# Value products of two attention groups from neighbouring tokens, the residue and class order made by a store and a load

## The reference

```python
def dilated_group(q, k, v, bias_table, window, dilation):
    # query t attends keys t - j*dilation, 0 <= j*dilation <= window
    ...
    s = jnp.einsum('brnqhe,brnkhe->brnhqk', qb, kb) * (E ** -0.5) + bias
    ...
    o = jnp.einsum('brnhqk,brnkhe->brnqhe', p, vb)
    o = o / den
...
for g, (window, dilation) in enumerate(DILATED_GROUPS):
    q, k, v = three projections of u for this group, 2048 columns each
    o, lse = dilated_group(q, k, v, table, window, dilation)
wts = softmax over the groups' lse
o = sum of wts * o;  y = o * silu(gate);  return y @ w_out
```

## Time and profile before

| | us |
|---|---|
| median of 3 timed runs (lowest, highest) | 1629.93 (1629.87, 1630.2) |
| profiled execution, whole | 1630.79 |
| its span | 1629.1 |
| TensorE busy with products | 1615.5 |
| TensorE busy with weight loads | 1372.4 |
| VectorE / ScalarE / GpSimd busy | 809.1 / 643.3 / 97.1 |

### The profile page before, as it was taken

One profiled execution on the slowest core, in us unless ns is written; L12 is line 12 of the kernel. 1 busy time (PEld: TensorE's weight loads), 2 busy tenths in 40 slices (PEclk: granted clock), 3 DMA queues, 4 the chain that ended last, 5 costly groups with the idle time before them and its releaser, 6 DMA issues.

```text
span 1629.1 us, 23054 instructions
## 1 busy us (share of the span) xinstructions
PE 1615.5 (99%) x8584; PEld 1372.4 (84%) x8584; DVE 809.1 (50%) x1452; ACT 643.3 (39%) x1096; POOL 97.1 (6%) x166
## 2 busy tenths in 40 slices
PE   9999999999999999999999999999999999999997
PEld 7888888888887998888998888898888889888886
DVE  6874674575677724444333444423344431443446
ACT  7553453453453533333232334332333332243332
POOL 5600000000000020000020000002000001000000
PEclk9999999999999999999999999999999999999999
DMA  6623223223221444333242343334423333433311
GB/s 181 185 81 98 77 77 95 85 77 90 78 78 52 122 125 97 84 83 84 65 142 79 96 97 84 71 102 118 96 62 89 94 71 104 133 95 86 83 50 65
DMA packets 251265, 151.99 MB, mean 93 GB/s; under 512 B 49536, under 2 KB 230352, under 8 KB 251184
## 3 DMA queue, kind: packets, MB, share of 16 engines
q1 hardware_dynamic: 204592, 138.95, 30.8%
q0 software_dynamic: 4592, 11.09, 2.0%
q10 hardware_dynamic: 42000, 0.79, 1.4%
HBM read 144.30 MB, written 5.71 MB: 92 GB/s over the span
## 4 chain that ended last, share of the span: by engine, by line
PE 97%; DVE 2%; ACT 1%; DMA 1%; issue 0%; DVEq 0%; ACTq 0%; SPq 0%
PE proj L475 81%; PE inner L794 3%; PE inner L475 3%; PE inner L742 1%; PE inner L777 1%; PE inner L760 1%; PE inner L658 1%; PE inner L681 1%; PE inner L684 1%; PE inner L670 1%; PE inner L663 0%; PE inner L756 0%; DMA ident<-consts 0%; DVE v L1702 0%; DMA stat_o<-residue_stats 0%; PE inner L691 0%
## 5 line engine op out<-in xcount | busy, mean ns | idle before, releaser
L1214 DVE TENSOR_TENSOR w_lo<-raw,w_hi 128x1024 fp32r<-128x1024 f32 x252 | 307.8, 1222 | 443.1 <-ACT w_hi L843 442.2
L475 PE MATMUL proj<-u_hi,w_hi 128*128 128x512 f32 x1280 | 509.5, 398 | 0.0
L475 PE MATMUL proj<-u_hi,w_lo 128*128 128x512 f32 x1280 | 499.6, 390 | 0.0
L475 PE MATMUL proj<-u_lo,w_hi 128*128 128x512 f32 x1280 | 498.5, 389 | 0.0
L843 ACT ACTIVATE w_hi<-raw 128x1024 fp32r<-128x1024 f32 x252 | 265.0, 1052 | 129.9 <-PE proj L475 116.7
L475 PEld LDWEIGHTS proj<-u_hi,w_lo 128*128 128x128 f32 x1280 | 240.2, 188 | 52.0
L475 PEld LDWEIGHTS proj<-u_lo,w_hi 128*128 128x128 f32 x1280 | 240.7, 188 | 48.0
L475 PEld LDWEIGHTS proj<-u_hi,w_hi 128*128 128x128 f32 x1280 | 240.5, 188 | 48.1 <-issue 0.3
L475 PE MATMUL proj<-w_hi,u_hi 128*128 128x512 f32 x440 | 176.9, 402 | 0.2 <-DVE u_lo L1278 0.2
L475 PE MATMUL proj<-w_hi,u_lo 128*128 128x512 f32 x440 | 173.6, 394 | 0.0
L475 PE MATMUL proj<-w_lo,u_hi 128*128 128x512 f32 x440 | 173.5, 394 | 0.0
(11 more groups left out here) (189 smaller groups left out, 1547.2 us busy)
## 6 DMA issues: line engine op xcount, KB each, us to landing
raw<-at_w_in SPq DMA_DIRECT2D x160, 512.0 KB, 4.3
raw<-hg_w_in SPq DMA_DIRECT2D x63, 512.0 KB, 4.1
raw<-hg_w_out SPq DMA_DIRECT2D x16, 512.0 KB, 3.6
raw<-at_w_out SPq DMA_DIRECT2D x16, 512.0 KB, 4.2
v<-rows POOLq DMA_DIRECT2D x64, 64.0 KB, 2.0
v<-x SPq DMA_DIRECT2D x4, 512.0 KB, 6.0
bias_tiles<-ext_rows POOLq DMA_DIRECT2D x1, 2048.0 KB, 11.1
bias_n<-bias_tiles POOLq DMA_DIRECT2D x16, 128.0 KB, 4.5
```

The lines of the kernel that those rows point to most:

```text
L475: ins = nc.tensor.matmul(bank[:, :], stationary(a), moving(b), start=(first and n == 0), stop=(last and n == 2))
L1214: nc.vector.tensor_tensor(w["lo"][:, slot, :], raw[:, slot, :], w["hi"][:, slot, :].bitcast(F32), ALU.subtract).then_inc(w_ready, 1)
```

## The change

The value products of all three groups take tokens 128s to 128s + 127. The order that groups 2 and 3 want is made afterwards: ScalarE writes each block to a row of `rows` (`staged`), GpSimd stores it to a DRAM tensor, in token order, and when a group's four blocks are stored, one transfer of 1 MB loads them with token 4i + r on partition i and in block r (group 2), or with the classes one behind the other (group 3). Since the RMS factor now goes by token for both groups, VectorE makes it in one order only. New waits: ScalarE's, for the store that last read the row; GpSimd's, for a group's four stores; and VectorE's, before it writes a quad's first logits over the rows.

```diff
+        turn_dram = nc.dram_tensor("value_rows", [GROUPS - 1, S, HQ * P], F32, kind="Internal").ap()
...
-        staged_v = rows[:, 8:10, :]
+        def staged(q, group, s):
+
+            if q is None:
+                return rows[:, 4 + s if group == 1 else 8 + s if s < 2 else 2 + s, :]
+            return rows[:, 8 + s % 2, :]
...
-            def move_classes(q):
-
+            turned = (None, turn_dram[0].rearrange("(i r) n -> i (r n)", r=RES),
+                      turn_dram[1].rearrange("(m c r) n -> c m (r n)", c=CLASSES, r=RES))
+
+            def turn_rows(q, group):
+
+                turn = 0 if q is None else q + 1
                 for s in range(ST):
-                    _, bank, filled = AT.event(q, 2 * ST + s + (0 if q is None else AT.heads))
+                    _, bank, filled = AT.event(q, ST * group + s + (0 if q is None else AT.heads))
                     wait_turn(pool, pool_met, bank_free[bank], filled + 1)
-                    for c in range(CLASSES):
-                        pool.dma_start(v_sb[2][c * MEM:(c + 1) * MEM, s, :], staged_v[c::CLASSES, s % 2, :])\
-                            .then_inc(v_moved[s % 2], 16)
-
-            move_classes(None)
+                    if q is not None and s == 0:
+                        wait_turn(pool, pool_met, v_loaded[group], turn * 16)
+                    pool.dma_start(turn_dram[group - 1, s * P:(s + 1) * P, :], staged(q, group, s))\
+                        .then_inc(v_stored[group][s], 16)
+                for stored in v_stored[group]:
+                    wait_turn(pool, pool_met, stored, (turn + 1) * 16)
+                pool.dma_start(v_sb[group][:, :, :].rearrange("p a b -> p (a b)"), turned[group]).then_inc(v_loaded[group], 16)
+
+            turn_rows(None, 1)
+            turn_rows(None, 2)
...
                 if not last:
-                    move_classes(q)
+                    turn_rows(q, 1)
+                    turn_rows(q, 2)
...
-                        cols = slice(s, S, RES) if group else slice(s * P, (s + 1) * P)
+                        cols = slice(s * P, (s + 1) * P)
...
-                cols = slice(s, S, RES) if group else slice(s * P, (s + 1) * P)
+                cols = slice(s * P, (s + 1) * P)
...
                 if h == 0:
-                    for moved in v_moved:
-                        pe.wait_ge(moved, (g // HQ + 1) * 2 * 16 * CLASSES)
+                    for loaded_rows in v_loaded[1:]:
+                        pe.wait_ge(loaded_rows, (g // HQ + 1) * 16)
...
-            def move_values(q, e, s, bank):
+            def stage_values(q, group, e, s, bank):
 
                 turn = 0 if q is None else q + 1
-                if s >= 2 or q is not None:
-                    act.wait_ge(v_moved[s % 2], (2 * turn + s // 2) * 16 * CLASSES)
-                nc.scalar.activation(staged_v[:, s % 2, :], value_bank(AT, q, e)[:, :], ACT.Copy).then_inc(bank_free[bank], 1)
+                if q is None and group == 2 and s >= 2:
+                    act.wait_ge(v_stored[1][s - 2], 16)
+                elif q is not None and s >= 2:
+                    act.wait_ge(v_stored[group][s - 2], (turn + 1) * 16)
+                elif q is not None and group == 1:
+                    act.wait_ge(v_stored[2][s + 2], turn * 16)
+                elif q is not None:
+                    act.wait_ge(v_stored[1][s + 2], (turn + 1) * 16)
+                raw_u = q is None and group == 1
+                nc.scalar.activation(staged(q, group, s), value_bank(AT, q, e)[:, :], ACT.Copy,
+                                     scale=cols[:, 8 + s:9 + s] if raw_u else 1.0).then_inc(bank_free[bank], 1)
...
-            picked = (y_f, eg)
-            for i, row in enumerate((rstd[:, :].rearrange("p (t n) -> p t n", t=ST),
-                                     rstd[:, :].rearrange("p (n r) -> p r n", r=RES))):
...
+            picked = y_f[:, :].rearrange("p (t n) -> p t n", t=ST)
+            nc.vector.tensor_tensor(picked, rstd[:, :].rearrange("p (t n) -> p t n", t=ST),
+                                    ident[:, :].unsqueeze(1).broadcast_to([P, ST, P]), ALU.mult).then_inc(rcol_step, 1)
...
+                        if i == K1 and h == 0:
+                            for loaded_rows in v_loaded[1:]:
+                                dve.wait_ge(loaded_rows, (q + 1) * 16)
```

More of the change, by code:

```diff
@@ L270, in program @@
         spread_out = sem("spread_out")
-        v_moved = [sem(f"v_moved{i}") for i in range(2)]
+        v_stored = [None] + [[sem(f"v{g}_stored{s}") for s in range(ST)] for g in range(1, GROUPS)]
+        v_loaded = [None] + [sem(f"v{g}_loaded") for g in range(1, GROUPS)]
         fin_T, fin_base, fin_sq, fin_step, fin_rstd, fin_ready = sems("fin_T fin_base fin_sq fin_step fin_rstd fin_ready")
@@ L850, in copy_values @@
                 raw_u = q is None and group < 2
-                if layer is AT and group == 2:
-                    move_values(q, e, s, bank)
+                if layer is AT and group:
+                    stage_values(q, group, e, s, bank)
                     return
                 nc.scalar.activation(v_sb[group][:, s, :], value_bank(layer, q, e)[:, :], ACT.Copy,
-                                     scale=cols[:, 8 + ST * group + s:9 + ST * group + s] if raw_u else 1.0)\
+                                     scale=cols[:, 8 + s:9 + s] if raw_u else 1.0)\
                     .then_inc(bank_free[bank], 1)
-            def move_values(q, e, s, bank):
+            def stage_values(q, group, e, s, bank):
                 turn = 0 if q is None else q + 1
-                if s >= 2 or q is not None:
-                    act.wait_ge(v_moved[s % 2], (2 * turn + s // 2) * 16 * CLASSES)
-                nc.scalar.activation(staged_v[:, s % 2, :], value_bank(AT, q, e)[:, :], ACT.Copy).then_inc(bank_free[bank], 1)
+                if q is None and group == 2 and s >= 2:
[9 more added lines that the diff above has]
+                                     scale=cols[:, 8 + s:9 + s] if raw_u else 1.0).then_inc(bank_free[bank], 1)
             def u_high(which, k):
@@ L1552, in _ @@
             dve.wait_ge(rstd_ready, 2)
-            picked = (y_f, eg)
-            for i, row in enumerate((rstd[:, :].rearrange("p (t n) -> p t n", t=ST),
-                                     rstd[:, :].rearrange("p (n r) -> p r n", r=RES))):
-                nc.vector.tensor_tensor(picked[i][:, :].rearrange("p (t n) -> p t n", t=ST), row,
-                                        ident[:, :].unsqueeze(1).broadcast_to([P, ST, P]), ALU.mult).then_inc(rcol_step, 1)
-            for i in range(2):
-                dve.wait_ge(rcol_step, i + 1)
-                ins = nc.vector.tensor_reduce(cols[:, 8 + ST * i:8 + ST * (i + 1)],
-                                              picked[i][:, :].rearrange("p (t n) -> p t n", t=ST), AX.X, ALU.add)
-            ins.then_inc(rcol_ready, 1)
+            picked = y_f[:, :].rearrange("p (t n) -> p t n", t=ST)
+            nc.vector.tensor_tensor(picked, rstd[:, :].rearrange("p (t n) -> p t n", t=ST),
+                                    ident[:, :].unsqueeze(1).broadcast_to([P, ST, P]), ALU.mult).then_inc(rcol_step, 1)
+            dve.wait_ge(rcol_step, 1)
+            nc.vector.tensor_reduce(cols[:, 8:8 + ST], picked, AX.X, ALU.add).then_inc(rcol_ready, 1)
             split_lo(AT, None, 3, False)
```

## The result

| | before | after |
|---|---|---|
| median of 9 runs, us (lowest, highest) | 1629.97 (1629.25, 1631.51) | 1636.5 (1630.14, 1638.61) |
| profiled execution, us | 1630.79 | 1630.14 |
| its span, us | 1629.1 | 1628.4 |
| TensorE busy with products / weight loads, us | 1615.5 / 1372.4 | 1611.1 / 1336.3 |

The changed kernel is slower: the ratio is 1.003, 95% interval 1.0022 to 1.0038 (the quotient of the two medians is 1.004). The forecast of 1624.1 (1623.0 to 1626.0, faster) was wrong in sign. The nine executions spread over 8.5 us, those of before over 2.3, and the profiled one is the shortest of the nine. So the profile can explain why even that one did not gain; it can't explain the other 6 us.

The account below looks back on a forecast made before the run. TensorE was taken as the bound, busy 1615.5 of 1629.1 us. Gains of 4.4 us in three quads and 1.4 ahead of the heads, 5.8 together, took the median from 1629.93 to 1624.1 us; range 1623.0 to 1626.0.

Parts of the forecast that it names:

- 768 x 8.5 ns: TensorE's value products of groups 2 and 3: each step 8.5 ns shorter with neighbouring tokens, 6.5 us at most.
- its share in the first blocks: First row blocks of groups: TensorE still waits for w_lo's chain, leaving 4.4 us in three quads and 1.4 ahead of heads.
- VectorE's shorter factors: VectorE ahead of rcol_ready: one product of 1.07 us and its reduction go; counted as nothing, at most some 2 us.
- rival (2): Partial gain: w_hi and w_lo hold every group's first block, or DMA traffic lengthens copies; 2 to 3 us lost, 1626.5; 6%.
- Second VectorE: VectorE's wait before first logits over staging rows: tightest ahead of the heads, costs nothing while the load arrives within 19 us.
- The store's landing: GpSimd's 256 KB stores of staged rows: landing taken as 2.2 us, like output stores, so ScalarE's copies lose nothing.
- rival (3): Slower: ScalarE stands behind the stores; a landing of 13 us gives 1638.5 us; 3%.
- Raw tiles have a lead of several tiles. I count nothing.: Raw weight tiles share DMA engines with the new stores and loads, an added 89 GB/s; counted as no cost.
- Third GpSimd: GpSimd waits for stores before issuing a load; queued stores and bias loads, and raw weights sharing DMA engines, counted as nothing.

Follow-up runs that it names:

- the pace alone: Kernel before with only the value products' addresses changed to neighbouring tokens, rows moved the old way: 1624.03 us against 1630.89, ratio 0.9960.
- the wait on stores: Changed kernel, but VectorE's wait before a quad's first logits is for the eight stores, not the two loads: 1630.58 us, ratio 0.9990.
- the two loads: Changed kernel with group 3's load issued as two loads of 512 KB, two classes each: 1633.95 us against 1630.04, ratio 1.0022.
- the step kept: Changed kernel, but products of groups 2 and 3 still read every fourth token: 1637.6 us against 1630.04, ratio 1.0060.
- the one with the extra transfer: Changed kernel with VectorE waiting for stores only, plus a second 512 KB transfer behind group 3's load to spare DRAM: 1627.07 us against 1630.63, ratio 0.9986.
- four loads: Changed kernel with group 3's 1 MB load issued as four, one per class, 32 partitions outermost: 1623.84 us, ratio 0.9961.
- the plain load: Changed kernel with group 3 loaded in group 2's order, 128 partitions outermost in the source: 1623.95 us, ratio 0.9959.
- both cures: Changed kernel with group 3's load as four by class and VectorE waiting for the stores, not the loads: 1623.98 us against 1630.63, ratio 0.9958.

## Why the prediction was wrong

**"768 x 8.5 ns", and its share in the first blocks.** Right. Loads of 188 ns, steps of 0.2267 us, TensorE held to 1.43 us a tile by the same chain at the start of group 2. In the profile 6.2 us were won, 6.9 in the kernel with the pace alone. The mechanism held and the size was slightly low: ahead of the heads 1.57 against 1.4, per quad 1.55 against 1.46. At the last tile of group 3 ahead of the heads the wait for w_lo came as forecast; the one at the second tile of quad 0 grew by 0.16 us (0.27 to 0.43) where I had 0.05. VectorE's shorter factors showed nowhere, and rival (2), a partial gain, did not come.

**"Second VectorE ... with 5.6 (half of what the 2 MB took, for 1 MB) ... even with 11.1 for the load".** This step failed. The threshold in it was right: "it costs nothing while the load is there in 19 us", and from the last copy, at 590.9, to the landing, at 621.5, it took 30.5 us, 11.7 of which VectorE stood. The size was not. Group 2's loads took 5.4 to 6.8 us, as I took; group 3's took 21.8 to 24.0. I bounded both by the 2 MB of the earlier trace rows as the nearest row, and asked only for its bytes. The two loads stand side by side in the change as `128x2048` and `128x1x2048`: for group 3 the source's slowest dimension is four classes. The experiments leave that as the cause: same bytes, queue and place with 128 or 32 partitions outermost take 5.5 and 8 us, with four 22 to 24, with two and half the bytes 22 to 24 until the last of the pair. The far bound of a cost has to come from a row of the same shape; where none has it, the bound was open, and the place with a threshold of 19 us was the one to price.

The Trainium skill says it. "DMA: Bandwidth & Descriptors", section "Why a DMA increments its semaphore by 16 and not by 1", lets a transfer use as many engines, up to 16, as divide the slowest dimension of both its patterns, and its "Rules for kernel authors" warn that an outermost dimension below 16 confines the whole transfer. By it the load had four engines: the traces agree, with 23.5% of 16 engines for its queue from 605 to 619 us, four late counts of 16 at its semaphore, and four times the time of group 2's load. Reading the change against that rule would have given the rival that happened, by an estimate from its rule and the 5.6 us that I took: 4 x 5.6 = 22 us for the load alone against 19 for copy, store and load.

The store's landing was too low as well (2.2 taken; 2.3/3.6/6.6 measured). No copy of ScalarE waited for one, so rival (3) did not come. But here the last store and its wait took 599.27 - 592.08 = 7.2 us where I had 2.75. So of the 19 us allowed, 4.4 more than planned went to the store and 16.6 more (22.2 for 5.6) to the load; the store alone would have stayed below the threshold.

**"Raw tiles have a lead of several tiles. I count nothing."** The lead was just enough in after: the longest landing of a tile rose from 14.1 us to 24.1 there and to 26.4, 27.5 and 27.8 in three profiles of the experiments; in layer 2, where the load stands, it was 11.1 to 12.4 without the confined load. In after ScalarE waited for two tiles, 4.2 us at most, and TensorE for none; where ScalarE waited 6.7 and 6.9 us, TensorE lost 0.9 and 1.2. What I also left out is that weights and values are not the only things that DMA engines bring. The kernels with a confined load have executions 4 to 10 us longer than their shortest: after (seven of nine from 1633.84 on), the wait on stores (seven of eleven), the two loads (six of ten from 1633.82 on), the step kept (two of six at 1645) and the one with the extra transfer (four of ten). The kernels whose loads use all engines (four loads, the plain load, both cures) had 15 executions within 1622.85 to 1625.01. That the confined load causes them is shown by that comparison. One profile of one kernel shows a late instruction block at the loop's jump as the whole of the 8.2 us; that the confined load held this block up is inferred from the time at which it came. For the longer executions of the other kernels, which no profile caught, the block is inferred from the like size. The mean granted clock, on record for each execution, fits: 0.995 to 0.997 in the seven longer ones of after and 0.997 to 0.998 in its two shorter ones. Between the start and the end of a span the clock falls in the profiles only in or right behind such a pause of TensorE, so it probably stood still in the longer ones too, but the clock does not tell for what; a weight tile some us later than the one that cost 1.2 us would do the same and is not excluded. Why it happens in some executions and not in others stays open.

So the median of after is: 1630.0 before, less 6.9 for the pace, plus 6.4 for VectorE's wait, plus 6 to 8 in most executions (read from the spread, not derived): 1635.5 to 1637.5, against 1636.5 measured. The rival on the slower side that I wrote had its mechanism at ScalarE's wait for the stores. What came is VectorE's wait for the load, which the prediction had dismissed under "Second VectorE", and the effect on other transfers, dismissed under "Third GpSimd". (The 89 GB/s given there for 4 MB in 45 us should be 93; nothing hangs on it.)

## What to carry to other kernels

Before a transfer gets a duration, write down the outermost dimension of its source and of its destination: here 128 and 32 were fast and 4 and 2 slow, at equal bytes in all. Splitting it so that the partitions come first costs a few more issues (here four of 0.5 us on an idle engine). It gave 7.3 us back between the shortest executions (1630.14 to 1622.85) and 13.6 at the median, each kernel taken against the kernel before on the same chip (6.5 above it and 7.1 below). Wait for what frees the buffer (the stores), not for what happens to come later (the loads), but cure the slow transfer first, since it also delays others: with the wait on the stores alone the median was still 1630.58, with the four loads 1623.84. When executions of one kernel fall into two clusters, a profile of the shorter one says nothing of the difference, and the fetch of instructions at a loop's jump belongs on the list.

## What the runs showed of the hardware

- A stationary operand read at a step of four fp32 elements loads in 308 to 333 ns (median 310), one of neighbours in 186 to 188, and back-to-back products of 512 columns go 0.2351 against 0.2267 us apart: 122 ns of load show as 8.5 ns of pace.
- A 1 MB load whose source had four outermost took 21.8 to 24.0 us in after and up to 27.0 in the experiments, with 128 outermost 5.2 to 7.5, and in four pieces of 32 at most 8.5. While it ran, tiles on another queue landed up to 24.1 us (after) to 27.8 us (the wait on stores, second profile) after their issue. Without it the longest in layer 2 is 11.1 to 12.4 us (before and four experiments); in layer 1 single tiles take up to 18.2 us without any such load.
- At the first jump back of the quads' loop TensorE stands for at most 0.6 us in the eleven other profiles, in some not at all, and stood for 6.25 us when the 16 KB instruction block came late. "Runtime: NRT & Kernel Launch" of the Trainium skill, section "Instruction fetch mechanics", says that each engine's sequencer fetches blocks of 16 KiB by its own DMA queue and that a taken branch outside the blocks at hand has to wait for one. The trace agrees: in the profiles of the experiment and of the kernel without the extra transfer the first product behind the jump starts 3.0 and 3.2 us after the start of the block. It adds the price of one that comes late: 6 us and the clock around it, 0.80, 0.50 and 0.85 in three windows of 4 us.
